# Two decoder layers: pre-norm factors applied to the projections' results, layers unrolled without a border, x and y in eight transfers

## The reference

```python
def rms_norm(x, g):
    xf = x.astype(jnp.float32)
    y = xf * lax.rsqrt(jnp.mean(xf * xf, axis=-1, keepdims=True) + NORM_EPS)
    return (y * g.astype(jnp.float32)).astype(x.dtype)

def conv_ffn(x, prev, lp):
    u = x @ lp["ffn_w_up"]
    gate, val = u[..., :D_FF], u[..., D_FF:]
    ext = jnp.concatenate([prev.astype(gate.dtype), gate], axis=1)
    conv = lp["ffn_conv_b"] + sum(ext[:, j:j + T] * lp["ffn_conv_w"][j] for j in range(CONV_WIDTH))
    h = jax.nn.gelu(conv) * val
    return h @ lp["ffn_w_down"], ext[:, -(CONV_WIDTH - 1):]

def layer_step(x, pos, nsa_fn, shift_prev, wkv_prev, conv_prev, lp):
    h = rms_norm(x, lp["norm_mix_pre"])
    proj = h @ lp["w_in"]
    ...
    mixed = jnp.concatenate([o_nsa.astype(x.dtype), o_rwkv.astype(x.dtype)], axis=-1) @ lp["w_out"]
    x = x + rms_norm(mixed, lp["norm_mix_post"])
    f, conv_new = conv_ffn(rms_norm(x, lp["norm_ffn_pre"]), conv_prev, lp)
    x = x + rms_norm(f, lp["norm_ffn_post"])
    return x, kv_rows, win_state, wkv_new, shift_new, conv_new
```

## Time and profile before

| | |
|---|---|
| executions | 2156.58, 2156.9, 2162.09 us; median 2156.9 |
| span of the profiled execution | 2160.4 us; its own time isn't given beside it |
| PE busy | 1962.7 us, 91% |
| DVE, ACT, POOL busy | 1231.5 (57%), 702.5 (33%), 49.3 us (2%) |
| mean granted clock of TensorE | 0.948 of full |
| DMA | 214.36 MB, 99 GB/s |

### The profile page before, as it was taken

One profiled execution on the slowest core, in us unless ns is written; L12 is line 12 of the kernel. 1 busy time (PEld: TensorE's weight loads), 2 busy tenths in 40 slices (PEclk: granted clock), 3 DMA queues, 4 the chain that ended last, 5 costly groups with the idle time before them and its releaser, 6 DMA issues.

```text
span 2160.4 us, 53488 instructions
## 1 busy us (share of the span) xinstructions
PE 1962.7 (91%) x22324; PEld 1809.6 (84%) x22324; DVE 1231.5 (57%) x2034; ACT 702.5 (33%) x1294; POOL 49.3 (2%) x137
## 2 busy tenths in 40 slices
PE   5999999888897999999679999999888889999995
PEld 5999887766696999999669988877667879999995
DVE  3254788888736444452333457888887264444423
ACT  3222334333433323242133124243334332232421
POOL 0000000000000110100000000000000000011000
PEclk9999899999997999999879998999999989999998
DMA  4224533243321222323132255231432212323232
GB/s 182 89 83 155 147 121 99 61 135 88 108 81 42 96 91 90 97 84 95 53 133 90 78 170 168 83 115 50 139 101 83 82 50 92 95 88 98 80 102 78
DMA packets 155835, 214.36 MB, mean 99 GB/s; under 512 B 21569, under 2 KB 121410, under 8 KB 153922
## 3 DMA queue, kind: packets, MB, share of 16 engines
q1 hardware_dynamic: 133250, 200.24, 29.5%
q10 hardware_dynamic: 22336, 10.62, 1.7%
HBM read 202.57 MB, written 16.59 MB: 101 GB/s over the span
## 4 chain that ended last, share of the span: by engine, by line
PE 64%; DVE 28%; issue 3%; ACT 2%; DMA 1%; SPq 1%; DVEq 0%; ACTq 0%; another core or an unknown queue 0%
PE ps L825 17%; PE ps L827 17%; PE ps L826 17%; DVE arena L2006 2%; PE ps L1177 2%; DVE arena L2015 2%; DVE hf_lo L1701 1%; DVE arena L1783 1%; DVE arena L1967 1%; DVE nsa L1943 1%; DVE arena L1920 1%; PE ps L844 1%; DVE ps L2005 1%; DVE nsa L1948 1%; PE ps L845 1%
## 5 line engine op out<-in xcount | busy, mean ns | idle before, releaser
L1694 DVE TENSOR_TENSOR ring_lo<-ring,ring_hi 128x1024 fp32r<-128x1024 f32 x202 | 247.4, 1225 | 681.2 <-ACT ring_hi L1335 680.9
L825 PE MATMUL ps<-hm_hi,ring_hi 128*128 128x260 f32 x1600 | 456.9, 286 | 9.7 <-DVE hm_lo L1701 4.9
L827 PE MATMUL ps<-hm_hi,ring_lo 128*128 128x260 f32 x1600 | 455.2, 285 | 0.0
L826 PE MATMUL ps<-hm_lo,ring_hi 128*128 128x260 f32 x1600 | 453.9, 284 | 0.0
L1335 ACT ACTIVATE ring_hi<-ring 128x1024 fp32r<-128x1024 f32 x202 | 213.8, 1059 | 677.1 <-PE ps L827 618.9
L825 PEld LDWEIGHTS ps<-hm_hi,ring_hi 128*128 128x128 f32 x1600 | 304.6, 190 | 12.8 <-issue 7.6
L826 PEld LDWEIGHTS ps<-hm_lo,ring_hi 128*128 128x128 f32 x1600 | 304.5, 190 | 0.0
L827 PEld LDWEIGHTS ps<-hm_hi,ring_lo 128*128 128x128 f32 x1600 | 304.4, 190 | 0.0
L825 PE MATMUL ps<-in_hi,ring_hi 128*128 128x260 f32 x736 | 212.9, 289 | 4.5 <-DVE ring_lo L1694 4.5
L825 PE MATMUL ps<-hf_hi,ring_hi 128*128 128x260 f32 x704 | 201.7, 287 | 9.5 <-DVE hf_lo L1701 8.2
L827 PE MATMUL ps<-in_hi,ring_lo 128*128 128x260 f32 x736 | 209.2, 284 | 0.0
(11 more groups left out here) (398 smaller groups left out, 3359.2 us busy)
## 6 DMA issues: line engine op xcount, KB each, us to landing
ring<-in_w SPq DMA_DIRECT2D x202, 512.0 KB, 3.5
extra<-in_kv_cmp SPq DMA_DIRECT2D x96, 128.0 KB
arena<-in_kv_cmp SPq DMA_DIRECT2D x80, 128.0 KB, 2.2
slot<-in_kv_cmp SPq DMA_DIRECT2D x80, 128.0 KB, 3.0
out_win_old<-in_win SPq DMA_DIRECT2D x16, 511.0 KB, 4.6
arena<-in_k_sel SPq DMA_DIRECT2D x72, 64.0 KB, 2.0
extra<-in_k_sel SPq DMA_DIRECT2D x72, 64.0 KB
slot<-in_v_sel SPq DMA_DIRECT2D x72, 64.0 KB, 2.1
```

The lines of the kernel that those rows point to most:

```text
L825: mmul(out, wh, hi[:, k, cols], start=(k == 0), stop=False)
L826: mmul(out, wh, lo[:, k, cols], start=False, stop=False)
L827: last = mmul(out, wl, hi[:, k, cols], start=False, stop=(ci == len(chunks) - 1 and k == k1 - 1))
L1694: v.tensor_tensor(ring_lo[:, n % RING, :], r, ring_hi[:, n % RING_HI, :], SUB).then_inc(S["w_lo"], 1)
```

## The change

- Norms 1 and 3 no longer change the operand. ACT splits x times the gain as the blocks come and squares each behind it (`scaled_split`); DVE forms the rest (`scaled_lo`). PE sums the squares between the two passes of the pair (`between`), and spreads the factor in the middle of the third tile (`middle`). The factor is multiplied into the results: by DVE, which now evacuates all tiles of the input projection and the FFN's gate tiles alone (`evac_scaled`), and into the convolution's GELU before its product with the value.
- The second pass of a pair takes one tile after the other, so the first releases its chunk earlier. The spreading uses all 128 rows (`quarter`), and its results lie in two banks instead of four.
- The second weight chunk of the FFN is split ahead of norm 2's copy.
- The loop over layers is written out in Python; the engines no longer meet. Semaphores go on counting or exist once per layer, and SP clears the rest in the first FFN. The gains of both layers have places of their own.
- x comes in eight transfers, two of them between the first weight chunks, y leaves in eight. Constants, LoRA weights and the shift state are loaded later.

```diff
-            with sp.Fori(0, DEPTH) as l:
+            for l in range(DEPTH):
+                S, before = SL[l], SL[l - 1] if l else None
                 def chunk(n):
                     if n >= RING:
                         sp.wait_ge(S["w_used"], n - RING + 1)
+                    elif before is not None:
+                        sp.wait_ge(before["w_used"], max(m for m in range(N_CHUNK) if m % RING == n) + 1)
                     sp.dma_start(ring[:, n % RING, :], I["w"][l, n]).then_inc(w_ready[n % RING], 16)
+                sp.dma_start(par[:, l, :], I["cols"][l]).then_inc(S["params"], 16)
                 for n in range(C_OUT):
+                    if l == 0 and n < 2:
+                        sp.dma_start(x[:, n, :], I["x"][n]).then_inc(x_ok[n], 16)
                     chunk(n)
+                    if l == 0 and n == 1:
+                        for k in range(2, KB):
+                            sp.dma_start(x[:, k, :], I["x"][k]).then_inc(x_ok[k], 16)
+                    if l == 0 and n == 2:
+                        sp.dma_start(pages[:], I["pages"]).then_inc(pages_in, 16)
+                        sp.dma_start(cst[:], I["consts"]).then_inc(const_ok, 16)
...
+                        sp.dma_start(prev_s, I["shift"][l].rearrange("p (a b) -> p a b", a=RP)).then_inc(S["lora_ok"], 16)
+                        sp.dma_start(lora, I["lora"][l]).then_inc(S["lora_ok"], 16)
...
-                host_meet(S["arrive"], list(S.values()) + list(T.values()) + w_ready + c_ready)
-            sp.dma_start(O["y"].rearrange("k p t -> p k t"), x[:]).then_inc(const_ok, 16)
+            for k in range(KB):
+                sp.wait_ge(SL[-1]["norm_h"], KB + k + 1)
+                sp.dma_start(O["y"][k], x[:, k, :]).then_inc(y_stored, 16)
...
+                    between()
                     for i, b in enumerate(banks):
+                        for k in range(KB):
+                            pe.wait_ge(S["s_lo"], SPLITS * l + first + k + 1)
+                            wh = ring_hi[:, (n + i) % RING_HI, k * P:(k + 1) * P]
+                            for h, cols in HALVES:
+                                last = mmul(ps[:, b + h, 0:HALF], wh, lo[:, k, cols], start=False, stop=(k == KB - 1))
+                        last.then_inc(S["w_used"], 1)
...
+                def norm_spread():
                     pe.wait_ge(S["norm_a"], norm_n[0])
+                    for q, out in enumerate(spread):
+                        last = mmul(out, quarter[:, q:q + 1].to_broadcast((P, P)), rows, start=True, stop=True)
                     last.then_inc(S["norm_b"], 1)
...
+                dense_pair(0, in_hi, in_lo, 0, lambda: norm(sq))
                 for m in range(2, N_IN):
+                    dense_tile([(m, 0, KB)], in_hi, in_lo, middle=norm_spread if m == 2 else None)
...
+                def scaled_split(dst, g, sq_dst, ready):
                     for k in range(KB):
+                        act.wait_ge(*ready(k))
+                        A(dst[:, k, :], x[:, k, :], ACT.Copy, scale=C(g, k)).then_inc(S["s_hi"], 1)
+                        A(sq_dst[:, k, :], x[:, k, :], ACT.Square).then_inc(S["norm_sq"], 1)
...
                 for m in range(2 * FT):
                     split_w(C_UP + m + 2)
+                    if m == 0:
+                        norm_root(3)
...
                     act.wait_ge(S["ffn_c"], FT * l + i + 1)
                     o.go(A(cv[:, i % 2, :], cv[:, i % 2, :], ACT.Gelu_apprx_tanh))
...
+                def evac_scaled(dst, rows=P):
+                    n = n_dense[0]
+                    dve.wait_ge(S["w_used"], tile_done(n))
+                    v.tensor_tensor(halves(dst), bank2(2 * (n % 3))[0:rows], halves(rs)[0:rows], MUL).then_inc(S["evac_v"], 1)
+                    n_dense[0] += 1
...
+                        v.scalar_tensor_tensor(dst[:, k, :], x[:, k, :], C(g, k), hi[:, k, :], MUL, SUB).then_inc(S["s_lo"], 1)
...
                 split_w(0, 1)
+                if before is not None:
+                    dve.wait_ge(S["stores"], STORES * l)
+                scaled_lo(in_lo, "mix_pre", in_hi)
                 norm_inv(1)
...
                 norm_inv(2)
+                split_w(C_UP + 1)
+                norm_out(2)
                 add_normed(hf, "mix_post")
-                split_w(C_UP + 1)
+                scaled_lo(hm_lo, "ffn_pre", hm_hi)
                 norm_inv(3)
...
                 for i in range(FT):
                     split_w(C_UP + 2 * i + 2)
+                    if i == 0:
+                        norm_out(3)
+                    n = n_dense[0]
+                    dve.wait_ge(S["w_used"], tile_done(n))
+                    if i >= 2:
+                        dve.wait_ge(S["ffn_t"], FT * l + i - 1)
+                    o.go(v.tensor_tensor(halves(gx[:, i % 2, 2:2 + TOK]), bank2(2 * (n % 3)), halves(rs), MUL))
+                    o.tell(S["evac_v"])
+                    n_dense[0] += 1
                     conv(i)
                     n = n_dense[0]
                     split_w(C_UP + 2 * i + 3)
+                    dve.wait_ge(S["ffn_act"], FT * l + i + 1)
+                    o.do(v.tensor_tensor(cv[:, i % 2, :], cv[:, i % 2, :], rs, MUL))
```

More of the change, by code:

```diff
@@ L856, in _ @@
[L856 to L870 removed]
+            pe.wait_ge(ones_ok, 1)
@@ L871, in norm_part @@
                     pe.wait_ge(S["norm_a"], norm_n[0])
-                    for r, out in zip(QROWS, spread):
-                        last = mmul(out, ones[r, :], rows[r, :], start=True, stop=True)
+                    for q, out in enumerate(spread):
+                        last = mmul(out, quarter[:, q:q + 1].to_broadcast((P, P)), rows, start=True, stop=True)
                     last.then_inc(S["norm_b"], 1)
-            pe.wait_ge(ones_ok, 1)
-            pe.wait_ge(const_ok, 48)
-            with pe.Fori(0, DEPTH) as _l:
-                dense_n[0] = norm_n[0] = 0
-                norm(sq)
@@ L1331, in split_w @@
                         if n < N_CHUNK:
-                            act.wait_ge(w_ready[n % RING], 16 * (n // RING + 1))
+                            act.wait_ge(w_ready[n % RING], landed(l, n))
                             if n >= RING_HI:
                                 act.wait_ge(S["w_used"], n - RING_HI + 1)
+                            elif before is not None:
+                                act.wait_ge(before["w_used"], max(m for m in range(N_CHUNK) if m % RING_HI == n) + 1)
                             A(ring_hi[:, n % RING_HI, :], ring[:, n % RING, :], ACT.Copy).then_inc(S["w_hi"], 1)
@@ L1655, in _ @@
             LD = -math.exp(-0.5)
-            dve.wait_ge(const_ok, 48)
-            o.do(v.tensor_scalar(onesblk[:], blk, 1.0 / HD, None, MUL))
-            o.do(v.tensor_scalar(pages[:], pages[:], 0, N_POOL - 1, MAX, ALU.min))
-            o.tell(pages_ok)
-            with dve.Fori(0, DEPTH) as _l:
-                dve.sem_clear(S["v_own"])
-                o.n = 0
+            o = Order(dve, counted["v_own"])
+            for l in range(DEPTH):
+                S, C, before = SL[l], columns(l), SL[l - 1] if l else None
                 n_dense = [0]
                 def norm_inv(n):
-                    dve.wait_ge(S["norm_mm"], n)
+                    dve.wait_ge(S["norm_mm"], 4 * l + n)
                     o.do(v.tensor_scalar(rows, ps[:, 6, 0:TQ], EPS, None, ADD))
@@ L1707, in _ @@
                 split_w(0, 1)
+                if before is not None:
+                    dve.wait_ge(S["stores"], STORES * l)
+                scaled_lo(in_lo, "mix_pre", in_hi)
                 norm_inv(1)
-                for k in range(KB):
-                    v.scalar_tensor_tensor(hm[:, k, :], x[:, k, :], C("mix_pre", k), rs, MUL, MUL).then_inc(S["norm_h"], 1)
-                split_s(in_lo, hm, in_hi, KB)
-                o.go(v.memset(pr[:, :, 0:1], 0.0))
-                o.go(v.memset(state[:], 0.0))
                 def beside(r):
```

355 lines of the change are left out of this document (165 added, 190 removed).

## The result

The changed kernel took 2117.61, 2118.16, 2120.87 and 2122.88 us, median 2119.51; the kernel before, now with a fourth run, has the median 2158.18. The medians lie 38.7 us apart; the ratio is 0.9817, 95% interval 0.9803 to 0.9832, which is 39.5 us. Measured again later with five runs, it was 0.9806 (0.9793 to 0.9819), 41.9 us. So the kernel is 1.8 to 1.9% faster, a difference well clear of the spread of the executions. The forecast was 43.5 us and 2113, the range 2103 to 2128.

What follows compares the result with a forecast made beforehand. With PE busy 91% of the span, only places where it stands still or runs slowly could be won; the terms summed to -43.5 us, giving 2113.4 us from the median, range 2103 to 2128.

Steps and rivals of the forecast that it cites:

- The start: First pair of the run: ends at 25.5 us instead of 38.7, -13.2 us.
- Before the FFN: Middle norm, each layer: the first FFN pair ends at 672.9 us instead of 680.3, a gain of 7.4 us.
- Behind the pair: FFN, each layer: new 4.2 us wait of PE for weight chunk 3, then 1.7 us of low clock; +3.0 us.
- Rival 3: FFN: the wait for weight chunk 3 does not appear; 5.9 us less per layer, 2101.6 us; chance 0.06.
- Between the layers: Border of the two layers: first product at 1079.2 us instead of 1098.0, second pass ends at 1096.3 instead of 1112.3; -16.0 us.
- Rival 5: Border: layers don't overlap, as ACT and DVE wait for every store of the first; 16.0 us lost, 2129; chance 0.01.
- The end: Last norm and y: y's last block leaves alone, span ends at 2155.6 us instead of 2160.4; -4.8 us.
- `hf_lo`: Last FFN pair: DVE's splits that PE waits for start 1.4 us later; +2.8 us in all.
- behind the input pairs: Behind both input pairs: waits of 0.55 and 0.2 us, a gain of 2.4 us each, -4.8 for two.
- Rival 1: First passes paced by ACT stay at 1.2 GHz: up to 4.5 us in three places, 2126 us; chance 0.12.
- Rival 2: Start and end: eight small transfers cost more than one; 8 and 10 us lost, 2131 us; chance 0.05.
- Rival 4: FFN pairs: DVE becomes the bound, PE waiting from 2.5 us more than now per pair; 2179 us at 4; chance 0.02.

Runs made afterwards that it cites:

- start: Changed kernel with both weight chunks issued ahead of x's blocks and one tiny ACT operation first to load its table early: 2119.09 us, ratio 0.9802.
- c1_mid: Changed kernel with ACT's split of the FFN's second weight chunk ahead of the middle norm's square root: 2116.77 us, ratio 0.9809.
- a1_chunk3: Changed kernel with the FFN's weight chunk 3 split ahead of the first GELU on ACT and the norm's copy and convolution on DVE: 2108.28 us, ratio 0.9765.
- extra5: Changed kernel with five more dummy products on DVE in each of the FFN's 44 pairs: 2192.78 us, ratio 1.0145 to the kernel before.
- h1_inter: Changed kernel with the second pass of each pair interleaved again, both tiles ending together: 2132.1 us, ratio 0.9868.

## Why the prediction was right, and where its sizes were off

**The mechanism** was right at each place that the prediction named, and so was the sign: what the change wins lies at the places where PE stood still, the start, the two middle norms, the border and the end, and nowhere in the 44 pairs, which still take 11.48 us.

**The start** (-13.2, measured -12.5). Two terms were off and partly cancelled. Landing: "issues and landing add 2.9" gave 7.0 us; the chunk took 6.03 us from its issue at 2.64, to 8.67, with two blocks of x issued ahead of it, and ACT's table load (1.28 us at 5.64) came only behind chunk 0's landing. The run start shows what both were worth: 1.1 to 1.5 us. Sums of squares: 0.24 us a block, the lower of the two bounds, where I took 0.37. That 1.1 us helped in each of the four pairs. A block in 1.15 us instead of 1.28 made no difference, as PE was the slower one.

**Before the FFN** (-7.4, measured -7.8 and -8.0). x's update started at 639.8, 4.5 us behind the spreading, as worked out; c1_mid confirms that the split of the second chunk is what lies between. **Behind the pair** (+3.0, measured +3.7 and +3.8): the wait was 4.4 us for 4.2, the one directly behind the pair 0.76 for 0.55, the low clock about 1.6 for 1.7, the spreading in tile 2 0.91 for 1.0. The 0.4 us that the sum gave the kernel before for a late chunk did not occur: its tile 3 began at 690.28, 0.12 us behind tile 2's last product. That a split behind the convolution is late by all of it was read from the order of the instructions, and a1_chunk3 won 11.3 us by undoing it. Rival 3 had fallen with the two waits of 4.4 us in the profile.

**Between the layers** (-16.0, measured -17.3). The first product came 11.8 us behind the update's start, forecast 11.95. The rest is the cheaper sums and a shorter pass, less 0.7 for the spreading, which costs 1.7 us at 1.2 GHz: eight products of 128 rows instead of 0.5 for those of 32 rows. I had counted it at one price; at the border and at the end it was dearer by 0.7. One row was misread: the prediction puts 0.3 us of waits for ACT into the first pass of the kernel before (10.7 us). There were none: its products came 0.22 us apart until 1104.2, so its length was the low clock. **Rival 5** was not seen: ACT's first block for the second layer was ready at 1054.0, while x's later blocks were still being updated.

**The end** (-4.8, measured -4.5), **`hf_lo`** (+1.4 a layer, measured +1.3), **behind the input pairs** (0.56 and 0.25 us of waiting for 0.55 and 0.2): as forecast.

**Rival 1** was not seen, for the reason that the prediction gives against it: first passes begin at 1.2 GHz and are at 2.4 GHz after 3 to 6 us (the run's first pass by the rate of its products), and until then PE has no gap between blocks. A block's eight products take 1.7 to 1.9 us there, so PE falls behind ACT's 1.28. At 2.4 GHz it mostly works off what has piled up; in the changed kernel it waits for at most the last block, by 0.1 us. So the rival's own case, 0.3 us of idle time in block after block, hardly arose, and what it would do to the clock stays open. The Trainium skill's case of a clock that falls again and again ("TensorE: Matmul & The Clock Gate", "A second HAM failure mode: psum-queue depth-cycling") does not occur in any of these passes: none fell again. **Rival 2**: eight pieces of y landed in 2.1 us each, the whole in 7.0. The Trainium skill's 1 MiB or more per DMA ("DMA: Bandwidth & Descriptors", "Rules for kernel authors"), a rule for the most bandwidth, would have led to the slower form here, because what counts is when the last byte lands behind its producer, not the rate. The 14 us that the prediction worked out from the Trainium skill's fixed 2.0 us ("Anatomy of one DMA"), a figure for DMAs that GpSimd issues (here SP issues them), did not appear. x's first three pieces landed at 3.98, 6.64 and 9.32 us, with the weight chunks between them, so more than 1 us apart, which the prediction had named as a sign of being wrong; the others came 0.7 us apart, and PE waited for none behind the first. **Rival 4**: the mechanism exists, its threshold was stated too low. The prediction says that PE waits "from 2.5 us more than now per pair" and counts 1.4; but 2.5 is what its own rows leave behind the two added products (12.6 - 10.1), and counted from before the change they give 12.6 - 8.7 = 3.9. Measured, 1.4 + 2.2 = 3.6 us more than before were free, and extra5, with 5.0, was slower than before.

**The total.** By profile 45.0 for a forecast of 43.5; by medians 38.7 and 41.9, so less than forecast. The prediction had noticed that its profile was of a long execution of the kernel before (span 2160.4) and took the same sum off the median. But the profiles differ by more than the medians also because the changed kernel's is of its fastest run, and in the second layer's merged phase the difference is 1.8 us larger than the change explains. That stretch varies by some us from execution to execution in every kernel here. What makes it vary was not looked into. That the sum came so close is in part luck: the sums of squares at their lower bound gave 4.4 us more than counted in four pairs, about as much as the other terms together gave less.

## What to carry to other kernels

- Where a factor is the same for all channels that a product sums over (a norm's root), it can go onto the result: PE can start on the raw blocks, and the root's chain runs beside the products. What then bounds the start is the next engine's order: list what stands ahead of the split that the first product needs.
- When a wait moves, look for what is queued behind it on the same engine. Here one weight split behind a convolution cost 11 us in two layers, and two behind an update 7.5; moving them into gaps where the engine mostly waited anyway cost 0.8 us at the border, which the 7.5 already count, and nothing that was seen in the FFN.
- Before two products go onto a helper engine, measure its slack by adding dummy ones: three fitted, five made the kernel slower than it had been.

## What the runs showed that was not expected

At the start of the run the granted clock stands at 1.00 while the products come at the rate of 1.2 GHz, 11 in 2 us, as in a stretch further on that shows 0.50:

```profile
12.00:14.00 2.00, 2.00 (x11) 2.00 (x11) 1.27 (x3) 2.00 (x5) 0.00 (x0) 1.00 1.05 434
...
1064.00:1066.00 2.00, 2.00 (x10) 2.00 (x10) 2.00 (x4) 0.00 (x0) 0.00 (x0) 0.50 0.00 0
```

There the count of products is the better witness. And the price of the same wait is not fixed: behind 4.4 us of waiting the low clock lasted 3.2 us in one kernel and 4.9 in another, and behind 2.2 us at the first pair it came in the kernel before and not in h1_inter. It varies where the kernels are alike too: behind the wait of 5.6 us for `hf_lo` in the first layer the products were back at 0.12 us after 2.95 us in the changed kernel's profile and after 5.95 in that of a1_chunk3, which changes nothing there. Such a stretch costs half its length, 1.6 us for 3.2 and 2.4 for 4.9, so one move's gain can be given back at the next wait, as in the profiled execution of c1_mid.
